# Issuing the next head's query unit in two runs of 24 matmuls instead of five parts

## The reference, cut to what matters

```python
def _diff_attention(xm, k_all, v_all, q_offset, w_q, q_g, lam_p, head_g, w_o, rel_bias, lam_init):
    q = _rms((xm @ w_q).reshape(B, T, A_HEADS, 2, A_DH), q_g) * (A_DH ** -0.5)
    ...
        s = jnp.einsum('bqhcd,bkhcd->bhcqk', qblk, k_all)
        ... # + bias, mask
        p = jax.nn.softmax(jnp.where(mask, s + bias, NEG_BIG), axis=-1)
        a = p[:, :, 0] - lam * p[:, :, 1]
        return jnp.einsum('bhqk,bkhe->bqhe', a, v_all)
    ...
    o = _rms(o, head_g) * (1 - lam_init)
    return (o.reshape(B, T, D_MODEL) @ w_o)
```

## Time and profile before

| | us |
|---|---|
| median of 3 runs (1498.41 to 1499.83) | 1498.81 |
| the profiled execution | 1501.64 |
| its span from first to last instruction | 1499.8 |
| TensorE busy | 1464.8 (98%) |
| VectorE busy | 950.1 (63%) |
| GpSimd busy | 758.1 (51%) |
| ScalarE busy | 419.0 (28%) |

### The profile page before, as it was taken

One profiled execution on the slowest core, in us unless ns is written; L12 is line 12 of the kernel. 1 busy time (PEld: TensorE's weight loads), 2 busy tenths in 40 slices (PEclk: granted clock), 3 DMA queues, 4 the chain that ended last, 5 costly groups with the idle time before them and its releaser, 6 DMA issues.

```text
span 1499.8 us, 30413 instructions
## 1 busy us (share of the span) xinstructions
PE 1464.8 (98%) x11892; PEld 1382.7 (92%) x11892; DVE 950.1 (63%) x1713; ACT 419.0 (28%) x895; POOL 758.1 (51%) x512
## 2 busy tenths in 40 slices
PE   5999999999999999999999999999999999999999
PEld 4998898999999999999999777778999999999999
DVE  4503465457774367776676257776975778567688
ACT  4302454221110011113211146665321223111142
POOL 2445333555555455555444534465655555556554
PEclk9999999999999999999999999999999999999999
DMA  9455423444456344453322342220222222222222
GB/s 368 143 186 171 141 71 114 148 148 157 166 177 222 100 141 166 144 183 116 106 75 74 93 161 87 87 85 31 85 85 84 80 95 78 85 79 76 88 97 102
DMA packets 57536, 183.58 MB, mean 122 GB/s; under 512 B 6441, under 2 KB 9905, under 8 KB 57441
## 3 DMA queue, kind: packets, MB, share of 16 engines
q1 hardware_dynamic: 54528, 179.34, 35.8%
q10 hardware_dynamic: 2912, 2.92, 0.6%
HBM read 171.69 MB, written 10.55 MB: 122 GB/s over the span
## 4 chain that ended last, share of the span: by engine, by line
PE 85%; DVE 4%; POOL 3%; DMA 3%; issue 2%; ACT 2%; SPq 0%; ACTq 0%; POOLq 0%; DVEq 0%
PE psum L730 60%; PE psum L786 7%; PE psum L991 4%; PE psum L1188 2%; POOL w_sum L688 2%; DMA raw<-in_w_down 2%; PE psum L741 1%; DMA ada_first<-in_ada_w 1%; PE psum L1280 1%; PE psum L1124 1%; PE psum L1243 1%; PE psum L1103 1%; DVE act_lo L1901 1%; PE psum L1230 1%; PE psum L929 1%
## 5 line engine op out<-in xcount | busy, mean ns | idle before, releaser
L613 POOL TENSOR_SCALAR w_hi<-raw 128x1024 fp32r<-128x1024 f32 (+1 forms) x168 | 192.5, 1146 | 583.8 <-PE psum L730 490.0
L617 POOL TENSOR_TENSOR w_lo<-raw,w_hi 128x1024 fp32r<-128x1024 f32 (+2 forms) x195 | 437.4, 2249 | 14.0
L730 PE MATMUL psum<-act_hi,w_hi 128*128 128x288 f32 (+1 forms) x1952 | 426.4, 299 | 0.2
L730 PE MATMUL psum<-act_hi,w_lo 128*128 128x288 f32 (+1 forms) x1952 | 420.0, 297 | 0.0
L730 PE MATMUL psum<-act_lo,w_hi 128*128 128x288 f32 (+1 forms) x1952 | 420.0, 296 | 0.0
L730 PEld LDWEIGHTS psum<-act_hi,w_hi 128*128 128x128 f32 x1952 | 315.6, 189 | 6.5 <-issue 2.7
L730 PEld LDWEIGHTS psum<-act_hi,w_lo 128*128 128x128 f32 x1952 | 315.7, 189 | 0.0
L730 PEld LDWEIGHTS psum<-act_lo,w_hi 128*128 128x128 f32 x1952 | 315.3, 189 | 0.0
L730 PE MATMUL psum<-hid_both,w_hi 128*128 128x288 f32 x704 | 122.6, 296 | 0.0
L730 PEld LDWEIGHTS psum<-hid_both,w_hi 128*128 128x128 f32 x704 | 103.6, 189 | 0.8 <-issue 0.8
L1848 DVE SCALAR_TENSOR_TENSOR psum<-ada_quad,cst,psum 128x512 f32<-128x512 f32 x144 | 96.9, 749 | 0.0
(11 more groups left out here) (365 smaller groups left out, 2393.3 us busy)
## 6 DMA issues: line engine op xcount, KB each, us to landing
raw<-in_w_stream SPq DMA_DIRECT2D x153, 512.0 KB, 3.5
ada_quad<-in_ada_w SPq DMA_DIRECT2D x48, 512.0 KB, 4.5
raw<-in_w_down SPq DMA_DIRECT2D x32, 704.0 KB, 4.3
ada_ring<-in_ada_w SPq DMA_DIRECT2D x32, 512.0 KB, 4.3
ada_first<-in_ada_w SPq DMA_DIRECT2D x8, 1024.0 KB, 14.2
line_rep<-line SPq DMA_DIRECT2D x8, 352.0 KB, 4.6
line<-line_rep SPq DMA_DIRECT2D x8, 352.0 KB, 5.3
x<-in_x SPq DMA_DIRECT2D x4, 576.0 KB, 5.6
```

The source lines that it names most:

```text
L613: pool.tensor_scalar(hi, src, 1.0, 0.0, ALU.mult, ALU.add).then_inc(hi_split, 1)
L617: last = pool.tensor_tensor(lo[:, c:c + w], src[:, c:c + w], hi[:, c:c + w].bitcast(F32), ALU.subtract)
L730: last = mm(psum[:, b + half, 0:n_cols], weights[wp][:, k, :], parts[ap][:, k, half * HT:half * HT + n_cols], start=(k == 0 and n == 0), s ...
```

## The change

In heads 1 to 5 the 48 matmuls of the query unit were dealt out over the five steps as 8, 8, 8, 12 and 12. They are now issued as 24 in step 0 (the first half of the tokens) and 24 in step 3 (the second half). VectorE's `query_first` moves from its step 2 to its step 1; `query_second` stays in step 4. Head 0 is as before: its unit has parts in front of the loop and in steps 1 and 2. No instruction is added or removed.

```diff
@@ TensorE, loop over g, after att_scores(g)
                 if p == 0 and s >= 1:
                     if s < 3:
                         query_part(2, 12 * s + 12, 12 * s + 24)
-                elif p + 2 < H and p >= 1:
-                    query_part(p + 2, *((0, 8), (8, 16), (16, 24), (24, 36), (36, 48))[s])
+                elif p + 2 < H and p >= 1 and s in (0, 3):
+                    query_part(p + 2, *((0, 24) if s == 0 else (24, 48)))
                 if s == 1 and p >= 1 and not late:
                     query_sums(p + 1)
@@ VectorE, loop over g, after att_score(g)
-                if s == (2 if p else 0) and p + 2 < H:
+                if s == (1 if p else 0) and p + 2 < H:
                     query_first(p + 2)
                 elif s == 4 and p + 2 < H:
                     query_second(p + 2)
```

## The result

| | before | after |
|---|---|---|
| median | 1499.22 (4 runs, 1498.41 to 1499.83) | 1513.28 (4 runs, 1508.89 to 1517.49) |
| the profiled execution | 1501.64 | 1517.49 |
| its span | 1499.8 | 1515.7 |
| mean granted clock of the four executions | 0.998 (the profiled one) | 0.990, 0.993, 0.995, 0.993 |

The change makes the kernel slower: ratio 1.0095, 95% interval 1.0075 to 1.0114, some 14 us. 1502.9 was predicted, in a range to 1505.2. The direction was right, the size was 3.5 times too small. The scatter is news too: the executions before lie within 1.4 us, those after within 8.6, and the slowest has the lowest mean clock.

What follows compares the result with a forecast made beforehand. TensorE was taken as the bound, with step 1's sums held by ScalarE's queue behind the turn. Heads 1 to 5 summed -0.20 + 0.93 + 0.63 + 0.93 + 1.78 = +4.07 us: 1502.9, range 1499.8 to 1505.2.

Steps and rivals of the forecast that it cites:

- the chain from the turn to the sums: Step 1's sums start 3.61 us after step 0's turn, whatever stands between; the gap at line 1201 grows to 1.7 us.
- Step 3 gains 12 and step 4 loses 12: 0 within 0.1: Moving 12 query matmuls from step 4 to step 3 changes a head's time by 0 within 0.1 us.
- the check of room: At step 4's turn in head 4, VectorE's weights are ready at 8.7 against 10.35 after the change, leaving 1.6 us.
- the 0.13 that I had booked as a gain of step 3: Step 3's 12 more matmuls cover the small wait at line 1258: between 0 and 0.3 us, 0.13 taken.
- Head 5: Later sums and scores +1.61, `query_first` leaving VectorE's stretch -0.36, VectorE meeting GpSimd +0.53: +1.78 us.
- +0.53: Head 5: VectorE's multiplication at line 2333 slides under GpSimd's work, 0.75 us against 1.28; bounds 0 and 1.06.
- A: Loss taken back at head 5's end, which then costs 0 to 0.5: sum +2.5 us, 1501.3; chance 0.20.
- D: No difference: TensorE's idle time at line 1201 only changes place; chance 0.05.
- B: Faster: squares hang on VectorE's maximum, not TensorE's turn, so longer runs cover the waits: -4.7 us, 1494.1; chance 0.07.
- C: VectorE becomes the bound in heads 2 to 4 too: +1.6 to +3 on top, 1504.5 to 1506; chance 0.08.

Runs made afterwards that it cites:

- the first run alone: Kernel before with 24 query matmuls in step 0, but still 12 in step 3 and 12 in step 4: ratio 1.0105, fastest execution 1508.17.
- the first of the two faster kernels: Kernel before with the sums of step 1 moved behind that step's turn and values in heads 1 to 4: 1495.24 against 1498.55, ratio 0.9973.
- the two halves of the change: Kernel before with only 24 in step 0 (12, 12 in steps 3, 4): ratio 1.0105; or with only 24 in step 3: 1501.64, ratio 1.0017.
- fill=6: Changed kernel with 6 useless matmuls more in the gap at line 1201 of heads 1 to 5: 1508.83, ratio 1.0057.
- the second faster kernel: Kernel before with step 1's sums behind turn and values in heads 1 to 4, and parts 16, 4, 4, 12, 12 in head 1: 1494.80, ratio 0.9967.
- the filled delay: Kernel before, ScalarE's squares done three times in heads 1 to 5, with 12 matmuls in the gap at line 1201: 1505.44 against 1499.21, ratio 1.004.

## Why the prediction was wrong, step by step

**Right: the chain from the turn to the sums.** Turn to sums is 3.61 us after the change as before it, the gap 1.7 us, and the first run alone costs 1.06 in head 4 with the clock held, as 8 matmuls are 1.07. The gaps are all at the upper end of the forecast (1.3 to 1.7 us), 8.6 us in all where some 7 was written.

**Wrong: "Step 3 gains 12 and step 4 loses 12: 0 within 0.1".** The step that failed is this one and the check of room that stood behind it. I asked only whether VectorE's weights would be ready at step 4's turn. That turn waits for ScalarE's line 1721 too, whose list puts it behind the copy that follows step 3's turn, the same construction that I had just priced in step 1. The chain of 3.13 us keeps some 2.3 us of work after the 12 matmuls leave. Measured by itself the move costs 0.6 us in each of heads 2 to 4. Without the clock the five heads cost +0.47, +1.66, +1.36, +1.66 and, up to head 6's turn, +2.23 us: 7.4 in place of 4.07. Of the 3.3 missing, each of heads 1 to 4 has 0.7: these 0.6 and the 0.13 that I had booked as a gain of step 3. Head 5 has the rest, 0.45.

**Missing: the clock.** No rival let it fall. The rows showed idle stretches of up to 1.21 us in the heads with the clock at 1.00, and I didn't ask what 1.7 would do. The trace of the kernel before had the warning at its start, where TensorE waits 2.4 us until 18.8 and 2.3 us until 32.2. The clock of the two stretches behind these waits was 0.84 and 0.83:

```profile
20.00:30.00 10.00, 8.88 (x272) 7.90 (x272) 7.18 (x20) 7.22 (x12) 0.64 (x1) 0.84 1.03 411
30.00:40.00 10.00, 7.83 (x163) 7.02 (x164) 4.09 (x12) 3.66 (x6) 0.00 (x0) 0.83 1.04 366
```

The Trainium skill (page "TensorE: Matmul & The Clock Gate", section "Part 1: The HAM clock gate") says that the engine's clock is gated by how busy it has been and has two levels; the traces agree, with 1.00 and 0.50.

The falls are 10.9 us of the profiled execution. At the median they are 14.1 - 7.4 = 6.7 by subtraction, nearly half of the result: an estimate, which takes the idle times of the profile for every execution. The two profiles differ by 15.9 us and not by 7.4 + 10.9 = 18.3, because the one before has a loss in the feed-forward block that the one after hasn't:

```profile
PE psum L997 <- POOL w_last L695: 2.5, 4, 1.3
```

It belongs to the execution and not to the order: of the other twelve profiles one has it too, the first of the two faster kernels. It is most of the 2.8 us by which the profiled execution before lies above the median.

**Head 5: the path right, one term too small.** +1.78 was forecast and +2.23 came. The scores of step 2 moved by 1.60 (forecast 1.61), VectorE's chain has no idle time from there to head 6's turn, and `query_first` left it. What was mis-sized is how much VectorE slows beside GpSimd: +0.53 was taken, between bounds of 0 and 1.06, and the instructions that ran while GpSimd's did took 0.99 us longer in all, 0.60 of it at line 2333 (1.35 us, 0.75 before). The new wait of 0.8 us at line 1258 isn't on this path: TensorE still waits 1.6 us for VectorE at head 6's turn.

**The rivals.** A (the loss taken back in head 5) and D (no difference) didn't happen. B (faster) is excluded by the constant 3.61 us. C (VectorE's chain) didn't happen in heads 2 to 4; what became late at step 4's turn was ScalarE. The upper end of the range had no room for a wait at step 4's turn in every head, and none for the clock.

## What to carry to other kernels

When work is moved out from under a wait, list every wait behind the place that it leaves and follow each back to where its chain starts: if it starts at an instruction of the same engine, its length is fixed, and whatever leaves it becomes idle time. Deal filler work by these chains, or move the waiting instruction behind work that has to be done anyway, which here gave 0.3% with no work saved. And price an idle stretch on TensorE not only by its length: count on a fall of the clock in some executions at the lengths that did it here, 1.5 us and up, or where two shorter ones come close together. A profile in which the clock held behind a gap doesn't clear that length. Look at the spread and the mean clock of the runs before you trust one profile.

## What was not expected of the hardware

- Gaps of 1.7 us between stretches of dense matmuls brought the clock to 0.50 in three of five heads in one execution of the changed kernel, in two of five in another, and in one of five with the first run alone; 0.7 us gaps in none of five. One fall cost from 1.6 to 6.1 us in this kernel. Filled with useless matmuls, the gap cost only its length: 1505.44 in place of 1515.96.
- The kernel before has such a gap too, which no version touches: 1.5 us at line 937, some 256 us into the span. In the profile before and seven others the clock holds behind it, in five it falls for some 3.5 us (the two halves of the change, `fill=6`, the second faster kernel and the filled delay). So a place that nobody changed can add to the scatter of any kernel here.
- Where the level returned differed as well: in head 3 of the first profile some 14 us later, in heads 2 and 4 after 7 and 4 us. What decides it, these runs don't show.
